# The first 128 tokens of two normed blocks go through two units' high weights and one unit's low weights ahead of the other tokens

## The reference, cut to what matters

```python
def rmsnorm(x, w):
    xf = x.astype(jnp.float32)
    y = xf * lax.rsqrt(jnp.mean(xf * xf, axis=-1, keepdims=True) + EPS)
    return (y * w.astype(jnp.float32)).astype(x.dtype)
...
    return _rmsnorm(x, final_norm)              # end of the first two layers
...
        h = rmsnorm(x, mix_norm[l])             # "norm 2", behind o_out
        proj = h @ w_mix_in[l]                  # segment g_qkv and others
...
        x = x + memory_xattn(h, mem_n, w_q, w_k, w_v, w_o)   # ends in segment x_out
        h = rmsnorm(x, ffn_norm[l])             # "norm 5", behind x_out
        x = x + conv_ffn(h, w_ffn_up[l], ffn_conv[l], w_ffn_down[l])   # f_up0, ...
```

## Time and profile before

| | |
|---|---|
| median of 3 runs | 2411.24 us (2410.8 to 2411.55) |
| the profiled execution's own time | 2411.45 us |
| its span, first to last instruction | 2409.7 us |
| TensorE busy | 2388.1 us, 99% of the span |
| DVE / ACT busy | 1629.7 us (68%) / 1178.4 us (49%) |
| DMA, mean of the span | 175 GB/s |

### The profile page before, as it was taken

One profiled execution on the slowest core, in us unless ns is written; L12 is line 12 of the kernel. 1 busy time (PEld: TensorE's weight loads), 2 busy tenths in 40 slices (PEclk: granted clock), 3 DMA queues, 4 the chain that ended last, 5 costly groups with the idle time before them and its releaser, 6 DMA issues.

```text
span 2409.7 us, 35511 instructions
## 1 busy us (share of the span) xinstructions
PE 2388.1 (99%) x14109; PEld 2066.5 (86%) x14109; DVE 1629.7 (68%) x2068; ACT 1178.4 (49%) x1439; POOL 157.9 (7%) x142
## 2 busy tenths in 40 slices
PE   8999999999999999999999999999999999999998
PEld 7888988898888888889988888988888888888887
DVE  6999776555685876696655446665777467755764
ACT  5433674544565654642654345545554334433433
POOL 1000000000200100000000000000212012200220
PEclk9999999999999999999999999999999999999999
DMA  8555546455436555553175555444565655555554
GB/s 251 189 195 186 164 140 214 147 180 171 158 108 207 166 183 177 183 167 106 37 253 176 199 186 164 141 175 161 190 203 179 208 175 194 189 194 191 183 180 143
DMA packets 337351, 422.45 MB, mean 175 GB/s; under 512 B 8494, under 2 KB 263228, under 8 KB 336716
## 3 DMA queue, kind: packets, MB, share of 16 engines
q1 hardware_dynamic: 334220, 410.87, 51.6%
q0 software_dynamic: 2544, 8.52, 1.1%
q10 hardware_dynamic: 464, 1.32, 0.2%
HBM read 418.53 MB, written 2.10 MB: 175 GB/s over the span
## 4 chain that ended last, share of the span: by engine, by line
PE 97%; DVE 1%; ACT 1%; DMA 0%; issue 0%; ACTq 0%; DVEq 0%
PE ps L759 36%; PE ps L760 18%; PE ps L816 10%; PE ps L818 10%; PE ps L817 10%; PE ps L763 1%; PE ps L764 1%; PE ps L762 1%; PE ps L1113 1%; PE ps L1105 1%; PE ps L1026 1%; PE ps L1030 1%; PE ps L855 0%; DVE h_cat L2343 0%; PE ps L1053 0%; DMA x<-in_x 0%
## 5 line engine op out<-in xcount | busy, mean ns | idle before, releaser
L759 PE MATMUL ps<-h_cat,w_hi 128*128 128x512 f32 x3824 | 1341.8, 396 | 5.4 <-DVE h_cat L2343 4.7
L760 PE MATMUL ps<-h_cat,w_lo 128*128 128x256 f32 x3824 | 1063.3, 278 | 0.0
L759 PEld LDWEIGHTS ps<-h_cat,w_hi 128*128 128x128 f32 x3824 | 717.0, 188 | 176.4 <-issue 8.3
L760 PEld LDWEIGHTS ps<-h_cat,w_lo 128*128 128x128 f32 x3824 | 719.4, 188 | 2.1 <-issue 1.9
L2200 DVE TENSOR_TENSOR w_lo<-ring,w_hi 128x2048 fp32r<-128x2048 f32 (+2 forms) x279 | 588.4, 2111 | 166.1 <-ACT w_hi L1417 163.1
L1417 ACT ACTIVATE w_hi<-ring 128x2048 fp32r<-128x2048 f32 (+2 forms) x279 | 493.0, 1767 | 87.6 <-PE ps L818 64.4
L2196 DVE TENSOR_TENSOR w_lo<-ring,w_hi 128x2048 fp32r<-128x2048 f32 (+1 forms) x136 | 302.8, 2232 | 231.2 <-ACT w_hi L1414 228.3
L1414 ACT ACTIVATE w_hi<-ring 128x2048 fp32r<-128x2048 f32 (+1 forms) x136 | 252.2, 1862 | 269.8 <-PE ps L818 239.6
L1435 ACT ACTIVATE stage<-ps 128x256 f32<-128x256 f32 x144 | 55.4, 384 | 400.1 <-PE ps L760 399.8
L816 PE MATMUL ps<-w_hi,h_cat 128*128 128x512 f32 x640 | 250.1, 391 | 0.0
L818 PE MATMUL ps<-w_hi,h_cat 128*128 128x512 f32 x640 | 249.2, 389 | 0.0
(11 more groups left out here) (466 smaller groups left out, 2335.2 us busy)
## 6 DMA issues: line engine op xcount, KB each, us to landing
ring<-in_w_ffn_up SPq DMA_DIRECT2D x44, 2048.0 KB, 8.0
ring<-in_w_mix_in SPq DMA_DIRECT2D x28, 2048.0 KB, 8.3
ring<-in_even_w_in SPq DMA_DIRECT2D x27, 2048.0 KB, 8.1
ring<-in_w_ffn_down SPq DMA_DIRECT2D x16, 2048.0 KB, 8.1
ring<-in_odd_w_in SPq DMA_DIRECT2D x11, 2048.0 KB, 9.3
ring<-in_even_w_out SPq DMA_DIRECT2D x8, 2048.0 KB, 8.2
ring<-in_odd_w_out SPq DMA_DIRECT2D x8, 2048.0 KB, 8.9
ring<-in_w_mix_out SPq DMA_DIRECT2D x8, 2048.0 KB, 8.2
```

The source lines that it names most:

```text
L759: mm(o[:, 0:2 * T], whi[slot][:, k, :], flat(cat[:, k]), start=first, stop=False)
L760: ins = mm(o[:, T:2 * T], wlo[slot][:, k, :], cat[:, k, 0, :], start=False, stop=end)
```

## The change

What runs on the first 128 tokens (`FRONT`) of the first four pairs of tiles (steps 0 to 7, `HALF_K` = 8) moves ahead, behind norms 2 and 5 (`AHEAD`):

- TensorE transposes row 0's tiles (8 transposes) inside the wide segment, behind row 1's second of four units, rather than behind its last.
- ACT writes their high halves there (`front_hi`, 8 operations of 128 columns, between its splits of weights), and DVE their low halves (`front_lo`, 8 operations of 128 columns).
- Behind row 1's last unit TensorE multiplies them by the high weights of units 0 and 1 (16 products of 2 × 128 columns) and by the low weights of unit 0 (8 products of 128 columns), `front_rows`. The calls with constants there go from 5 to 1 behind norm 2 and from 4 to 0 behind norm 5.
- The units then take only tokens 128 to 255 (`BACK`) in steps 0 to 7: unit 0 in both products, unit 1 in the high one (its low weights still take all 256 tokens).
- DVE splits unit 1's low weights in two halves of 1024 columns (`split_part`), the first before row 1's add, the second behind `lo` of pair 7. Before, the whole split stood ahead of the add.
- `hi` and `lo` of pairs 0 to 3 shrink from 256 to 128 columns.

```diff
+    AHEAD = {2: ("g_qkv", 0), 5: ("f_up0", 4)}
+    HALF_K = 8
+    FRONT, BACK = slice(0, P), slice(P, T)
...
+        def front_rows(norm):
+
+            name, first = AHEAD[norm]
+            g = S[name]
+            pe.wait_ge(sem["half_ready"], first + 4)
+            for j in range(2):
+                before, at = seg_of_narrow[g.f0 + j - ACC]
+                pe.wait_ge(*emptied(before, at + 1))
+                pe.wait_ge(sem["hi_ready"], g.n0 + j + 1)
+                for k in range(HALF_K):
+                    mm(two_of(bank(g, g.n0 + j))[:, :, FRONT], whi[(g.n0 + j) % WHL][:, k, :], h_cat[:, k, :, FRONT],
+                       start=(k == 0), stop=False)
+            pe.wait_ge(sem["lo_ready"], g.n0 + 1)
+            for k in range(HALF_K):
+                mm(bank(g, g.n0)[:, T:T + P], wlo[g.n0 % WHL][:, k, :], h_cat[:, k, 0, FRONT], start=False, stop=False)
...
+                if begun is not None and step < HALF_K:
+                    mm(two_of(o)[:, :, BACK], whi[slot][:, k, :], cat[:, k, :, BACK], start=False, stop=False)
+                    rows_of = BACK if j == 0 else slice(0, T)
+                    ins = mm(o[:, T + rows_of.start:2 * T], wlo[slot][:, k, :], cat[:, k, 0, rows_of], start=False, stop=end)
...
+                        if turned is not None and (t, j) == (1, g.units - 3):
+                            for p in range(4):
+                                turn_half(turned, p, 0).then_inc(sem["half_turned"], 1)
...
-                for p in range(4):
-                    turn_half(norm, p, 0)
-                for n in range({1: 4, 2: 5, 5: 4}[norm]):
-                    mm(ps[n % 2][:, 0:T], ident[:], causal[:, 0:T], start=True, stop=True)
+                if norm in AHEAD:
+                    front_rows(norm)
+                else:
+                    for p in range(4):
+                        turn_half(norm, p, 0)
+                for n in range({1: 4, 2: 1, 5: 0}[norm]):
+                    mm(ps[n % 2 + (2 if norm in AHEAD else 0)][:, 0:T], ident[:], causal[:, 0:T], start=True, stop=True)
...
+            if k in AHEAD:
+                split_to(S[then].n0 + 2)
+                front_hi(k)
             split_to(S[then].n0 + 3)
...
+        def front_hi(k):
+
+            for p in range(4):
+                act.wait_ge(sem["half_turned"], AHEAD[k][1] + p + 1)
+                for kk in range(2):
+                    ins = af(h_hi[:, 2 * p + kk, FRONT], turn_bank(k, p)[:, kk * T:kk * T + P], ACT.Copy,
+                             scale=col(NORMS[k], 2 * p + kk))
+                ins.then_inc(sem["half_hi"], 1)
...
+        def split_part(g, n, part_):
+
+            slot, c = n % WHL, g.c0 + (n - g.n0) // g.per_chunk
+            u0, k = ((n - g.n0) % g.per_chunk) * P, slice(8 * part_, 8 * part_ + 8)
+            dve.wait_ge(sem["hi_ready"], n + 1)
+            tt(wlo[slot][:, k, :], chunk(c % RING, g)[:, k, u0:u0 + P], whi[slot][:, k, :].bitcast(F32), ALU.subtract)\
+                .then_inc(sem["lo_ready" if part_ else "lo_front"], 1)
...
-            split_to(S[then].n0 + 2)
+            if k in AHEAD:
+                split_to(S[then].n0 + 1)
+                front_lo(k)
+                split_part(S[then], S[then].n0 + 1, 0)
+            else:
+                split_to(S[then].n0 + 2)
             add_row(g, 1)
...
             for b in range(4, 8):
                 lo(k, b)
+            if k in AHEAD:
+                g = S[AHEAD[k][0]]
+                split_part(g, g.n0 + 1, 1)
+                st["split"] = g.n0 + 2
```

More of the change, by code:

```diff
@@ L729, in highs_first, with two_of, unit @@
             ins.then_inc(sem["acc_ready"], 1)
-        def unit(g, j, n, i=None, rhs=None, tiles_ready=None, norm=None, read=None):
+        def two_of(o):
+            return o[:, 0:2 * T].rearrange("p (a t) -> p a t", a=2)
+        def front_rows(norm):
[12 more added lines that the diff above has]
+                mm(bank(g, g.n0)[:, T:T + P], wlo[g.n0 % WHL][:, k, :], h_cat[:, k, 0, FRONT], start=False, stop=False)
+        def unit(g, j, n, i=None, rhs=None, tiles_ready=None, norm=None, read=None, begun=None):
             slot, m = n % WHL, width(g, j)
@@ L738, in unit @@
                 return
-            pe.wait_ge(*((sem["first_lo"], 1) if i is None and n == 0 else (sem["lo_ready"], k0 + 1)))
+            late_rest = begun is not None and j == 1
+            if late_rest:
+                pe.wait_ge(sem["lo_front"], AHEAD[begun][1] // 4 + 1)
+            else:
+                pe.wait_ge(*((sem["first_lo"], 1) if i is None and n == 0 else (sem["lo_ready"], k0 + 1)))
             if i is not None:
@@ L782, in seg @@
                 unit(g, j, g.n0 + j, None, rhs, tiles_ready if j == 0 else None, norm if j == 0 else None,
-                     read if j == g.units - 1 else None)
+                     read if j == g.units - 1 else None, norm if norm in AHEAD and j < 2 else None)
                 if j == 0 and name in ("g_qkv", "x_k", "f_up0"):
@@ L822, in wide_unit, with wide_seg @@
                 ins.then_inc(sem["acc_ready"], 1)
-        def wide_seg(name, cat=None, tiles_ready=None, act0=None, first=0, norm=None, rows_apart=False, tile=None):
+        def wide_seg(name, cat=None, tiles_ready=None, act0=None, first=0, norm=None, rows_apart=False, tile=None, turned=None):
             g = S[name]
@@ L1094, in _ @@
         pe.wait_ge(sem["masked"], A_ODD + DSA_HEADS)
-        wide_seg("o_out", tiles_ready=H_GROUPS["gate"], first=3, tile=gate_tile, rows_apart=True)
+        wide_seg("o_out", tiles_ready=H_GROUPS["gate"], first=3, tile=gate_tile, rows_apart=True, turned=2)
         turn_first(2)
@@ L1387, in _ @@
         head_values(3)
-        wide_seg("x_out", tiles_ready=H_GROUPS["xattn"], first=2, rows_apart=True)
+        wide_seg("x_out", tiles_ready=H_GROUPS["xattn"], first=2, rows_apart=True, turned=5)
         turn_first(5)
@@ L1626, in hi @@
             b = turned_tiles(k, p)
+            rows_ = slice(P if k in AHEAD and p < 4 else 0, T)
             for kk in range(2):
-                ins = af(h_hi[:, 2 * b + kk, :], turn_bank(k, p)[:, kk * T:(kk + 1) * T], ACT.Copy,
+                ins = af(h_hi[:, 2 * b + kk, rows_], turn_bank(k, p)[:, kk * T + rows_.start:(kk + 1) * T], ACT.Copy,
                          scale=col(NORMS[k], 2 * b + kk))
             ins.then_inc(sem["ht_hi"], 1)
+        def front_hi(k):
[5 more added lines that the diff above has]
+                ins.then_inc(sem["half_hi"], 1)
         def norm(k, source, roots, free):
@@ L1866, in _ @@
         root_of(0, 3, "half_std", 1)
+        split_to(S["g_qkv"].n0 + 2)
+        front_hi(2)
         split_to(S["g_qkv"].n0 + 3)
@@ L2341, in lo, with front_lo @@
             b = turned_tiles(k, p)
+            rows_ = slice(P if k in AHEAD and p < 4 else 0, T)
             for kk in range(2):
-                ins = stt(h_lo[:, 2 * b + kk, :], turn_bank(k, p)[:, kk * T:(kk + 1) * T], col(NORMS[k], 2 * b + kk),
-                          h_hi[:, 2 * b + kk, :].bitcast(F32), ALU.mult, ALU.subtract)
+                ins = stt(h_lo[:, 2 * b + kk, rows_], turn_bank(k, p)[:, kk * T + rows_.start:(kk + 1) * T], col(NORMS[k], 2 * b + kk),
+                          h_hi[:, 2 * b + kk, rows_].bitcast(F32), ALU.mult, ALU.subtract)
             ins.then_inc(sem["ht_ready"], 1)
+        def front_lo(k):
+            for p in range(4):
+                dve.wait_ge(sem["half_hi"], AHEAD[k][1] + p + 1)
+                for kk in range(2):
+                    ins = stt(h_lo[:, 2 * p + kk, FRONT], turn_bank(k, p)[:, kk * T:kk * T + P], col(NORMS[k], 2 * p + kk),
+                              h_hi[:, 2 * p + kk, FRONT].bitcast(F32), ALU.mult, ALU.subtract)
+                ins.then_inc(sem["half_ready"], 1)
+        def split_part(g, n, part_):
[4 more added lines that the diff above has]
+                .then_inc(sem["lo_ready" if part_ else "lo_front"], 1)
         def scaled(k, source, c):
@@ L2726, in _ @@
         scaled(2, x, 1)
-        split_to(S["g_qkv"].n0 + 2)
+        split_to(S["g_qkv"].n0 + 1)
+        front_lo(2)
+        split_part(S["g_qkv"], S["g_qkv"].n0 + 1, 0)
         add_row(S["o_out"], 1)
```

7 lines of the change are left out of this document (5 added, 2 removed).

## The result

The changed kernel takes 2422.56 us (median of 6 runs, 2419.87 to 2423.49), the kernel before 2411.39 beside it (6 runs, 2410.8 to 2412.75): a ratio of 1.0042, 95% interval 1.0031 to 1.0054. It is 11 us slower, and the range forecast ended at 2412.0. The profiled execution took 2422.86 us, 11.41 more than that of before.

A forecast was written before the change was run, and what follows sets the result against it. The prediction took TensorE, busy 2388.1 of 2409.7 us, as the bound. Gains of 0.9 us at norm 5 and 0.65 at norm 2, together 1.55, took 2411.24 to 2409.7 us; range 2408.0 to 2412.0.

The forecast's parts named there:

- step 5: Unit 1 on TensorE: 8 high products at 0.12 for 0.23 us, gain 0.9 a norm; second half split ready in time.
- Step 6: Unit 2 waits for DVE's sum of unit 0: cost 0.15 us at norm 5, 0.45 at norm 2.
- Rival C: Behind the norms: with fewer constants the clock falls to 1.2 GHz during unit 0, about 2421 us; chance 3%.
- Step 1: Row 0's transposes move into row 1's wide products and delay row 1's chain: cost 0.95 us a norm.
- Step 2: Front halves on ACT and DVE stay hidden ahead of row 1's add, by 0.2 to 0.25 us: cost 0.
- rival A: Front halves on ACT and DVE cost more than priced and delay row 1's add: 2413.3 us; chance 22%.
- Step 3: `front_rows` behind row 1's last wide product takes 2.8 us; row 1's transposes slightly late at norm 5: cost 0.05.
- Step 4: Unit 0 shortens as ACT, DVE and TensorE each do less: gain 1.15 us a norm, bounds 0.85 and 1.5.
- rival B: Short operations at lower bounds, no wait at unit 2, 128-column product at 0.06: 2408.3 us; chance 9%.

The follow-up runs named there:

- experiment 1: The changed kernel with unit 1's low weights split whole, ahead of row 1's add; 2414.59 us, ratio 1.0016.
- experiment 4: The kernel before with only unit 1's split in two halves, the second behind the last low half; 2421.89 us, ratio 1.0044.
- experiment 9: The changed kernel with unit 0's constants call behind unit 1 and the second half split ahead of low halves of pairs 4 to 7; 2409.4 us.
- experiment 3: The changed kernel with eight calls of constants ahead of unit 3 behind both norms; 2421.14 us, ratio 1.0038.
- Experiment 11: The kernel before with fewer calls of constants, 5 to 1 behind norm 2 and 4 to 0 behind norm 5; 2414.52 us, ratio 1.0013.
- experiment 2: The changed kernel with the second half of unit 1's split right behind row 1's scaling, in DVE's gap; 2414.24 us, ratio 1.0015.
- Experiment 8: The changed kernel, constants call behind unit 1, unit 1's split whole ahead of the add (norm 2), second half in DVE's gap (norm 5); 2408.16 us.
- experiment 5: As experiment 1, with the call of constants behind unit 0 of g_qkv and f_up0 moved behind unit 1; 2408.72 us, ratio 0.9989.
- experiment 10: The changed kernel with only the call of constants behind unit 0 moved behind unit 1; 2421.11 us, ratio 1.0048.
- experiment 7: The kernel before without the call of constants behind unit 0 of g_qkv and f_up0; 2415.65 us, ratio 1.0015.

## Why the prediction was wrong

**The step that failed is step 5**, in its sentence "Its second half of low weights is ready 1.22 after the last low half, long before step 8." It is true (800.29 against the first product of step 8 at 802.34), and it answers the wrong question. It asks when TensorE needs the low weights, and not what else waits for the same count: SP's refill of the ring. Step 6 repeated it: "Queued behind that sum are the convolution of unit 0 and the split of unit 4, which unit 3 and later ones have microseconds to spare for." They had some, but the split of unit 4 waited for data that were 14.0 us late, not for DVE. The prediction never read SP's row. Read with ACT's, it would have given the price: the data land 14.2 us late (794.74 to 808.93), less 6.9 to spare is 7.3, and the table load is 7.4 later in the trace (801.64 to 809.02); ACT's split, DVE's split and unit 1's sum follow, and unit 3, which before had 2.9 us to spare behind that sum (809.72 to 812.57), loses 4.0 us. The prediction's last sentence does name "a wait behind unit 2 that DVE's later order brings about", but with no price and no part in the range. Experiments 1 and 4 show this as the cause, and 9 gives the dose: with 3.8 us less of lateness TensorE no longer waits.

**Rival C had the size (2421) but not the way.** Its clock was to fall behind the norms, for lack of constants. It stayed up there (1.00 from 784 to 796) and fell inside the wait ahead of unit 3, or 1.0 us behind it at norm 5; experiment 3 shows that the wait brought it down, by keeping it up without mending the wait. That the two sizes agree is luck. Experiment 11 speaks for C's mechanism where nothing takes the constants' place: the clock fell in its profiled execution, and the mean clock was lower in the other nine too. This agrees with how the prediction read the Trainium skill (TensorE: Matmul & The Clock Gate, Part 1: throttled is the default state, activity releases it): fewer constants are harmless as long as other products stand there. It isn't the whole of it: in experiment 4, with all constants in place, the clock fell at the start of unit 0 behind an idle of 1.43 us, which left it up in the kernel before, and in experiment 2, with the front rows, it fell in 3 executions of 10.

**The pace was in no step.** 2.4 us of the loss in the profiled execution, and some 5.6 in experiments 1 and 2, come from units at 5.66 us. The earlier trace rows hold only the fast value. But the trace of before has the slow one too, in shorter segments: units of 5.65 us stand there at 544 to 561, at 957 to 969 and at 1469 to 1486, with the clock at its upper level. Read over the whole trace rather than at the two norms, it would have shown that a unit has two prices.

**Steps 1 to 4 held, and what 5 and 6 say of TensorE.** TensorE and then DVE at norm 5 of the changed kernel:

```profile
1673.67 2.08 PE L747 MATMUL ps<-h_cat,w_hi 128*128 128x256 f32 x16
1675.58 1.01 PE L751 MATMUL ps<-h_cat,w_lo 128*128 128x128 f32 x8
1676.43 0.42 PE L904 MATMUL ps<-ident,xs 128*128 128x128 f32 x2
...
1678.36 0.35 PE L787 MATMUL ps<-h_cat,w_hi 128*128 128x256 f32 x1 [0.86 <-DVE h_cat L2397]
1678.56 0.22 PE L789 MATMUL ps<-h_cat,w_lo 128*128 128x128 f32 x1
1678.62 0.33 PE L787 MATMUL ps<-h_cat,w_hi 128*128 128x256 f32 x1
1678.79 0.22 PE L789 MATMUL ps<-h_cat,w_lo 128*128 128x128 f32 x1
```

```profile
1670.03 2.16 DVE L2406 SCALAR_TENSOR_TENSOR h_cat<-ps,prm,h_cat 128x128 fp32r<-128x128 f32 x8 [0.95 <-ACT h_cat L1679]
1672.11 1.21 DVE L2415 TENSOR_TENSOR w_lo<-ring,w_hi 128x1024 fp32r<-128x1024 f32 x1
1673.87 0.69 DVE L2439 TENSOR_TENSOR x<-x,ps 128x512 f32<-128x512 f32 x1 [0.55 <-PE ps L850]
```

- Step 1: row 0's transposes cost 0.87 us with the switch; forecast 0.95.
- Step 2: row 1's add stands 0.20 behind the last product's end of issue (1673.67), with 0.55 us idle ahead of it, 0.52 behind norm 2. The front halves are hidden by more than the 0.2 forecast, and rival A did not happen: an operation of 128 columns took 0.27 us on DVE and on ACT.
- Step 3: `front_rows` takes 1676.43 − 1673.67 = 2.76 us; forecast 2.8. 16 products at 0.12 and 8 at 0.106 (0.85 / 8).
- Step 4: unit 0's first product comes 1.41 us behind ACT's first high half (1676.95), forecast 1.4; the last low half is done 7.4 behind it, forecast 7.7. A step of unit 0 takes 0.23 us (1678.56 to 1678.79), which is 0.12 + 0.11, so rival B's 0.06 for a low product of 128 columns falls: halving its columns saved nothing but the 0.01 forecast. (The starts alone mislead: 0.06 behind the low product and 0.17 behind the high one. Only the pair can be priced.)
- Steps 5 and 6, as far as TensorE goes: unit 1 took 4.9 us (its first product at 800.25, its last low one at 805.05, and 0.12), 0.2 of it the switch behind the constants; forecast 4.7. The idle ahead of unit 2 was 0.31 us behind norm 2 (805.17 to 805.48), forecast 0.45, and nothing behind norm 5, forecast 0.15.

Together 1.4 us gained behind norm 5 (forecast 0.9) and 1.2 behind norm 2 (0.65), 2.6 in all, where 1.55 was forecast. The term that was too small is step 4's: behind norm 5 unit 0 starts 0.48 us earlier against the last wide product (4.69 for 5.17) and unit 1 follows 7.06 behind it for 8.08, 1.5 together, which is its upper bound, for 1.15. Experiment 8, which keeps the front rows and has none of the lateness, measures 2.6 us too.

## What to carry to other kernels

An instruction that moves later delays everything that its semaphore releases: list the waiters of the count, DMA queues first, and compare the lateness with the transfer's spare time, here 14.0 us late, where 10.2 (experiment 9) were still hidden from TensorE. A wait of TensorE named after an engine is only the last link; follow it back through ACT and DVE until a DMA issue or a busy engine stands there. Where a change should have paid and didn't, compare the starts of corresponding units: a step is a wait, a slope is a pace.

## What was unexpected in the hardware

The same stream of products (512 and 256 columns in turn, clock at the upper level) settles into one of two paces, 0.347 or 0.353 us a pair (579 or 567 products in 100 us), and keeps it to the end of the segment. The two differ in form: the starts of high products are 0.343 and 0.350 us apart in turn in the fast pace, and 0.349, 0.350 and 0.361 in the slow one, again and again. Which one it takes changed with one call of constants placed one unit earlier or later (experiments 1 and 5), with a wait ahead of it (behind norm 2 in the changed kernel and in 4 and 10, slow in all three, while behind norm 5 the same wait left the fast one), and it was fast in one segment of experiment 7 where it was slow in the other. What selects it stays open; it is worth 2.4 to 3.3 us a segment here.

The clock did not follow the length of an idle stretch alone: it fell behind 1.43 us ahead of unit 0 (experiment 4, norm 2) and stayed up behind the same 1.43 us in the kernel before; behind 3.12 us of idle ahead of unit 3 it fell (experiment 4, norm 5), behind 3.68 us it stayed up (experiment 10, norm 5), behind 3.77 it was down for 6.8 us and behind 3.61 for 3.4 (the changed kernel, norms 2 and 5). What decides was not tested.
